# A fused two-block transformer kernel: the first projection's opening group in another order and in smaller tiles

## What is computed

```
h = rmsnorm(x, norm_mix[layer])
(q, kc, vc, ks, vs, kw, vw, nsa_g, rq, rk, rv, rg, gate_a, gate_b) = jnp.split(
    h @ w_in[layer], offsets, axis=-1)
```

## Time and profile before

| what | value |
|---|---|
| median of three runs | 968.85 us |
| the profiled execution's own time | 968.41 us |
| its span, from the first to the last instruction | 966.6 us |
| TensorE busy | 958.8 us, 99% |
| VectorE busy | 625.5 us, 65% |
| ScalarE busy | 517.0 us, 53% |
| bytes moved | 170.37 MB, mean 176 GB/s |
| TensorE's granted clock | 1.00 over the span |

### The profile page before, as it was taken

The page is one execution under the profiler, slowest core; times in us unless marked ns, Lnnn a source line. Parts: engine busy times, 40 slices in busy tenths (PEclk is TensorE's granted clock), DMA queues, the critical chain, the costliest instruction groups (busy, mean ns, idle before and its releaser), DMA issues.

```text
span 966.6 us, 15946 instructions
## 1 busy us (share of the span) xinstructions
PE 958.8 (99%) x6548; PEld 869.1 (90%) x6548; DVE 625.5 (65%) x811; ACT 517.0 (53%) x785; POOL 58.1 (6%) x110
## 2 busy tenths in 40 slices
PE   9999999999999999999999999999999999999997
PEld 7877889989988898999988999998998899999996
DVE  5778685777555555778857787776554466555544
ACT  5576554555445444556865665545455445444443
POOL 2000001001000000304000002100000010000001
PEclk9999999999999999999999999999999999999999
DMA  9974536556656566466564465555645347565661
GB/s 303 310 240 127 146 88 176 160 168 203 210 176 190 181 192 194 119 196 195 148 184 142 121 185 186 165 185 172 197 153 170 113 153 218 178 198 175 195 192 45
DMA packets 135528, 170.37 MB, mean 176 GB/s; under 512 B 7856, under 2 KB 99296, under 8 KB 135456
## 3 DMA queue, kind: packets, MB, share of 16 engines
q1 hardware_dynamic: 133488, 165.20, 55.6%
q10 hardware_dynamic: 1424, 2.84, 0.8%
q0 software_dynamic: 544, 1.31, 0.5%
HBM read 168.28 MB, written 1.05 MB: 175 GB/s over the span
## 4 chain that ended last, share of the span: by engine, by line
PE 98%; DVE 1%; issue 0%; ACT 0%; POOLq 0%; DVEq 0%; POOL 0%; ACTq 0%
PE ps L367 15%; PE ps L368 15%; PE ps L369 15%; PE ps L398 8%; PE ps L399 8%; PE ps L400 8%; PE ps L350 5%; PE ps L724 5%; PE ps L725 5%; PE ps L723 5%; PE ps L448 3%; PE ps L479 1%; PE ps L481 1%; PE ps L480 1%; PE ps L613 1%; PE ps L645 1%
## 5 line engine op out<-in xcount | busy, mean ns | idle before, releaser
L1524 DVE TENSOR_TENSOR parts<-raws,parts 128x1024 fp32r<-128x1024 f32 (+2 forms) x309 | 367.7, 1207 | 231.3 <-ACT parts L1020 230.6
L1020 ACT ACTIVATE parts<-raws 128x1024 fp32r<-128x1024 f32 (+2 forms) x309 | 316.2, 1040 | 238.5 <-PE ps L369 137.5
L367 PE MATMUL ps<-room_r,parts 128*128 128x256 f32 x1248 | 352.2, 282 | 0.0
L368 PE MATMUL ps<-room_r,parts 128*128 128x256 f32 x1248 | 348.5, 279 | 0.0
L369 PE MATMUL ps<-room_r,parts 128*128 128x256 f32 x1248 | 348.3, 279 | 0.0
L367 PEld LDWEIGHTS ps<-room_r,parts 128*128 128x128 f32 x1248 | 234.6, 188 | 5.6 <-issue 3.9
L368 PEld LDWEIGHTS ps<-room_r,parts 128*128 128x128 f32 x1248 | 234.7, 188 | 1.3
L369 PEld LDWEIGHTS ps<-room_r,parts 128*128 128x128 f32 x1248 | 234.6, 188 | 0.0
L398 PE MATMUL ps<-parts,room_r 128*128 128x512 f32 (+1 forms) x336 | 134.8, 401 | 0.5 <-DVE parts L1524 0.5
L400 PE MATMUL ps<-parts,room_r 128*128 128x512 f32 (+1 forms) x336 | 131.1, 390 | 0.0
L399 PE MATMUL ps<-parts,room_r 128*128 128x512 f32 (+1 forms) x336 | 131.0, 390 | 0.0
(11 more groups left out here) (225 smaller groups left out, 875.7 us busy)
## 6 DMA issues: line engine op xcount, KB each, us to landing
raws<-in_w_in SPq DMA_DIRECT2D x99, 512.0 KB, 4.4
raws<-in_w_ffn_in SPq DMA_DIRECT2D x44, 512.0 KB, 4.2
raws<-in_w_up SPq DMA_DIRECT2D x32, 512.0 KB, 4.4
raws<-in_w_down SPq DMA_DIRECT2D x32, 512.0 KB, 4.3
raws<-in_w_ffn_out SPq DMA_DIRECT2D x22, 512.0 KB, 4.2
raws<-in_w_xkv SPq DMA_DIRECT2D x16, 512.0 KB, 4.3
raws<-in_w_out SPq DMA_DIRECT2D x8, 512.0 KB, 4.4
raws<-in_w_up_ssd SPq DMA_DIRECT2D x8, 512.0 KB, 4.6
```

The source lines that it names most:

```text
L367: e.matmul(ps, wh, hT[0][:, k, :], start=k == 0, stop=False)
L368: e.matmul(ps, wh, hT[1][:, k, :], start=False, stop=False)
L1020: e.activation(t.h, t.raw, ACT.Copy).then_inc(s["hi"], 1)
L1524: e.tensor_tensor(t.l, t.raw, t.h.bitcast(F32), ALU.subtract).then_inc(s["lo"], 1)
```

## The change

`tm` is no longer used for the opening group. A new generator, `opening`, makes the same 48 products in six tiles, of depths 1, 1, 1, 1, 2, 2. In each tile the order is: rounded by rounded for t = 0, the rest of x by rounded for t = 0, rounded by rounded for t = 1, the rest of x for t = 1, and then rounded x by the weights' rest for both t. In tile 0 the rest of x for t = 1 comes last of all. Each kind has its own wait, so a rounded product waits for `hi` and `xT_hi` alone. `x_half(1)` comes after three tiles (three chunks) where it came after two. On ScalarE and VectorE one more tile comes before the second half of `x`, and VectorE's rest of chunks 4 and 5 moves behind the rests of the second half of `x`. On SyncE the transfers of the second half of `x` stay behind chunks 0 to 3, now behind tile 3, and chunks 4 and 5 are now tile 4, which has to wait for a landing buffer. The numbers in `w1_behind` go up by one, so that each part stays behind the same weights.

```
+            def opening(w, depths):
+                own = [bank(), bank()]
+                toks = [slice(t * P, t * P + P) for t in range(2)]
+                k0 = 0
+                for deep in depths:
+                    w_ = weight(w[k0 * P:(k0 + deep) * P, 0:512], deep, 512)
+                    chunks_of = range(k0, k0 + deep)
+                    def rounded(t):
+                        need(s["hi"], w_.i + 1)
+                        for k in chunks_of:
+                            need(s["xT_hi"], (1 if k < 4 else 3) + t)
+                            e.matmul(psum[:, own[t], :], xT[0][:, k, toks[t]], w_.h[:, k - k0, :], start=k == 0, stop=False)
+                    def x_rest(t):
+                        for k in chunks_of:
+                            x_ready(MIX)(k, t)
+                            last = e.matmul(psum[:, own[t], :], xT[1][:, k, toks[t]], w_.h[:, k - k0, :], start=False, stop=False)
+                        return last
+                    def w_rest(t):
+                        need(s["lo"], w_.i + 1)
+                        for k in chunks_of:
+                            last = e.matmul(psum[:, own[t], :], xT[0][:, k, toks[t]], w_.l[:, k - k0, :], start=False, stop=k == 7)
+                        if k0 + deep == 8:
+                            ends(last, ("qkv", 0, t), own[t])
+                        return last
+                    rounded(0)
+                    x_rest(0)
+                    rounded(1)
+                    if k0 == 0:
+                        w_rest(0)
+                        w_rest(1)
+                        w_.release = done(x_rest(1))
+                    else:
+                        x_rest(1)
+                        w_rest(0)
+                        last = w_rest(1)
+                        w_.release = count if k0 + deep == 8 else done(last)
+                    k0 += deep
+                    yield
...
-            units = tm("qkv", w_in, 0, 512, xT, x_ready(MIX), depths=[1, 1, 2, 2, 2])
-            next(units)
-            next(units)
+            units = opening(w_in, [1, 1, 1, 1, 2, 2])
+            for _ in range(3):
+                next(units)
             x_half(1)
...
             rounds(MIX, 0, True, (1,))
-            round_tile()
-            round_tile()
+            for _ in range(3):
+                round_tile()
             e.dma_start(cols[:, 8:], a["cols"][:, 8:]).then_inc(s["cols"], 16)
             round_tile()
             rounds(MIX, 1, True)
...
             rests(MIX, 0, (1,))
+            for _ in range(3):
+                rest_of_tile()
+            gains(MIX, 1, True)
+            rests(MIX, 1)
             rest_of_tile()
-            rest_of_tile()
-            gains(MIX, 1, True)
-            rest_of_tile()
-            rests(MIX, 1)
...
-            w1_behind = {7: 0, 9: 1, 11: 2, 12: 3, 17: 4, 18: 5, 19: 6, 21: 7}
+            w1_behind = {8: 0, 10: 1, 12: 2, 13: 3, 18: 4, 19: 5, 20: 6, 22: 7}
...
-                if t.i == 2:
+                if t.i == 3:
```

More of the change, by code:

```diff
@@ L513, in mixed_ready @@
                 return lambda k, t=1: need(s["mixT"], 4 * u + k // 2 + 1)
+            zeros = junk[:, 0:P]
             def idle(n):
-                zeros = junk[:, 0:P]
                 for _ in range(n):
```

## The result

The changed kernel takes 970.6 us (median of 20 runs, 970.11 to 971.56) against 968.78 (20 runs): 1.8 us more, a ratio of 1.0017 with a 95% interval of 1.0011 to 1.0024. The forecast was 968.4 with a range of 967.7 to 969.5, so the time lies outside it, on the slow side.

What follows compares the result with a forecast made beforehand. Prediction: TensorE's own stream sets the time. Gains of 0.57 (first product) and 0.25 (chunk 4), less 0.43 (new wait), make 0.39, so 0.4 off the median of 968.85: 968.4, range 967.7 to 969.5.

Steps and rivals of the forecast that it cites:

- The first product: Opening group: starts at 7.21 when the idle products end, not 7.96; gain 0.57 us, from 0 to 0.75.
- The transposes and chunks 4 and 5: Opening group: transposes at 11.70; chunks 4 and 5 land at 12.0, and TensorE loses about 0.43 us on their rest.
- the net gain: Start of chunks 6 and 7: 0.57 + 0.25 - 0.43 = 0.39, so 0.4 us sooner, at 17.2.
- The sign of being wrong: Profile after: chunks 4 and 5 rounded after 12.3, first product near 7.5 or later, or new TensorE wait between 25 and 42.
- The extra waits and the split: TensorE's some ten extra waits cost 0 (bound 0 to 0.8 us), and chunks 2 and 3 as two tiles cost nothing.
- After the group ... Cost 0: After the opening group: block 1's transfer 0.9 us later stays just inside a slack of 1.26, so it costs 0.
- So an earlier start is kept to the end: After the opening group: TensorE's list of waits holds nothing for a transfer or rest, so nothing gained is lost.
- the downstream rival: Block 1's transfer over 1.3 to 1.8 us later delays angle reduction and next weights; 3 us later gives 970.0; chance 0.05.
- Late landing of chunks 4 and 5: Rival, opening group: landing at 12.9 and not 12.0 costs 0.86 us more, giving 969.3; chance 0.2.
- the fixed cost of a split transfer: Rival, chunks 2 and 3: the extra transfer puts 2.6 us in series, giving 969.65 (969.05 by the skill's figure); chance 0.04.

Runs made afterwards that it cites:

- order_only: The kernel before with the new order of products alone, its five tiles, queues and transposes as before; 968.56 us, ratio 0.9998.
- split_alone: Changed kernel with chunk 3 in chunk 2's buffer, transposes after two chunks, chunks 4 and 5's rest before x's rests; 968.45 us.
- hold: order_only plus a wait of SyncE for the first tile's rest before it issues chunks 4 and 5; 968.77 us, ratio 0.9998.
- tiles_only: The changed kernel with the old order of products, six tiles and all queues as changed; 972.44 us, ratio 1.0034.
- shared_landing: The changed kernel with chunk 3 landing in the second half of chunk 2's buffer, so chunks 4 and 5 are issued without a wait; 970.55 us.
- w1_later: The changed kernel with four 512 KB parts of the first compression weight behind tiles 13, 15, 16, 17, not 8, 10, 12, 13; 969.59 us.
- x_after_two: The changed kernel with the transposes of x's second half after two chunks in place of three; 970.41 us, ratio 1.0017.
- late_rest: order_only with VectorE's rest of chunks 4 and 5 moved behind the rests of x's second half; 969.16 us, ratio 1.0002.

## Why the prediction was wrong, step by step

- **The first product**: forecast 7.21, measured 7.14. It waited 0.44 for the rounding after all, since the idle products had ended by 6.7 in this execution and not at 7.45. The time was right; that the wait would be below 0.1 was not.
- **The transposes and chunks 4 and 5**: landing forecast 12.0, rounding started at 12.17; rounding of x at 13.13 (13.05); the products with the tile's rest forecast at 16.1 to 16.2, measured 16.26; chunks 6 and 7 forecast at 17.2, measured 17.30. Right, though the net gain was 0.28 and not 0.4. The sign of being wrong that did come is the last one, a new wait of TensorE between 25 and 42 us.
- **The extra waits and the split**: forecast 0, and order_only and split_alone show 0 within what can be measured.
- **The step that failed is "After the group ... Cost 0".** It went wrong in three places. First, I moved the issue of the transfer that ended at 23.49 by 0.9 and took its time to landing as fixed; it was issued 1.04 later (17.37) and took 8.1 and not 7.1, because what stood ahead of it had also lost time in the hole. So it landed 2.05 later. Second, I saw two late issues and did not add up what they left unmoved: 0.6 and 1.6 of engine time less the 0.3 made good between them, or 0.67 MB by 18 us, in front of a stretch with a share of 1.05 to 1.07, in which it is not made good. hold shows that the first hole alone would have been; the second, from the late rest, has no room behind it. I had the row for such a share and used it only to show that a fixed cost is hidden. Third, I took the slack from the wrong pair of rows, the angle reduction against the table load (1.26). The chain that is bound by transfers runs on through the last tile of the first matrix, the table load and the next matrix's first tile, and its slack was 0.54. Sum: that tile's rest is 1.95 late, less 0.54 of slack is 1.41, and the product starts 0.14 after the rest is ready (38.03 + 1.23 = 39.26 against 39.40): 1.55 behind, as measured.
- **"So an earlier start is kept to the end"** was the second thing taken from the list of waits, and it is not so: a list of waits shows nothing of slacks. In split_alone TensorE is 0.71 ahead at the next matrix and meets new waits near 57 and 617 us.
- **The rivals**: the downstream rival named the place and the direction, with 970.0 at 3 us later and a chance of 0.05. Its cause, a transfer that comes too late, was right, but not its path: the angle reduction ended at 33.56 + 0.51 = 34.07 in the changed kernel and the table load began at 35.22, so it still had 1.15 of slack. The threshold was 0.54 and not 1.3 to 1.8, and the chance belonged far higher, as the stretch is full of transfers. Late landing of chunks 4 and 5 and the fixed cost of a split transfer were not what happened: the landing was at 12.1, x's second half came in no later than before, and split_alone costs nothing. The section of the Trainium skill that the prediction cites there is on transfers issued by GpSimd; these are issued by SyncE, and no run here shows its 2 us as a price of the split.
- **Open**: the last 0.5 between the two profiled executions. It lies in two stretches in which TensorE's products follow each other by 1% less closely: 154 products from 547 us on take 17.97 in the trace of before and 18.14 in that of the changed kernel, 207 from 620 us on take 24.26 and 24.48. In a third, 146 from 683 us on take 17.03 in both, but 17.20 in seven other traces. Each of the fourteen traces has one of two values in each stretch, with five tiles as with six (order_only has 18.14, 24.26 and 17.20, tiles_only 17.97, 24.48 and 17.03), so this differs between executions and is not the change's. What sets it was not found. Also open is a wait of 0.3 for a tile near 618 us in tiles_only, shared_landing, w1_later, x_after_two and split_alone: five of the seven kernels with six tiles have it, none of those with five.

## What to carry to other kernels

Where the transfer queues are full for a long stretch, what has not been moved when it begins counts against the tightest slack behind it: add up the idle engine time that late issues make, less what is made good before the stretch, and do not shift one transfer by its issue. A buffer is given back by the step that reads it last; moving that step behind others on its own engine here also moved a transfer four tiles on. And take the slack at the end of the stretch that is bound by transfers, from the first tile that the bottleneck engine needs, not from a side chain.

## What the runs showed of the hardware

- A pause of TensorE of 2.07 us was followed by 3.1 us at a granted clock of 0.50, products 0.42 apart and not 0.23 (tiles_only); pauses of 0.87 and 1.09 us (late_rest, changed) were not: the mean granted clock stayed at 1.00 and the products behind them started 0.31 and then 0.23 apart. The Trainium skill (TensorE: Matmul & The Clock Gate, Part 1) has the two levels; the trace agrees.
- The landing of a 512 KB transfer came 4.0 us after its issue at 37.3 in before, 4.3 after the issue at 7.84 and 3.7 after that at 16.24 in the changed kernel, and 8.1 in the full stretch (issue at 17.37), so a time to landing can't be carried from one place in the queue to another.
- The same 154 products took 17.97 us in ten of the traces and 18.14 in four, 1% longer, with a granted clock of 1.00 in both cases.
